# Weight remainders of an odd projection on VectorE, a decay root without a reciprocal, and modulation panels streamed at other places

## The reference, cut to what matters

```python
def sublayer(x, shift, scale, gate, g_pre, g_post, fn):          # 4 of them: two layers, mixer and feed-forward
    h = rmsnorm(x, g_pre) * (1 + scale[:, None]) + shift[:, None]
    return x + gate[:, None] * rmsnorm(fn(h), g_post)

shift, scale, gate, ... = split(silu(cvec) @ mod_w[l] + mod_b[l], 6)   # 2 x (1024 x 6144)

# layer 0: h @ w_in_even (1024 x 3072) -> qa ka va qb kb vb; differential attention (a) and
#          neighbourhood attention (b), both with 128 cached keys; @ w_out_even; SwiGLU (2816)
# layer 1: h @ w_in_odd (1024 x 3088) -> q k v o gates xd gd
q, k = split(silu(conv_centred(qk, conv_c)), 2)
hc = rmsnorm(mlstm(q, k, v, gates), norm_g) * sigmoid(o)         # 4 heads, forward and backward
xc = conv_centred(xd, conv_d) + conv_d_b
# rglru(xc), forward and backward:
r  = sigmoid(xb @ wa + ba);  ig = sigmoid(xb @ wx + bx)
log_a = -8 * r * softplus(-lam);  a = exp(log_a)
u = sqrt(-expm1(2 * log_a)) * (ig * x)
h[t] = a[t] * h[t-1] + u[t]
out = concat([hc, (rf + rb) * gelu(gd)]) @ w_out_odd             # then a mixture of 8 SwiGLU experts, top 2
```

## Time and profile before

| | |
|---|---|
| three runs | 1744.79 us median, 1743.28 to 1745.66 |
| profiled execution | 1746.09 us, of it span 1744.5 |
| busy | TensorE 1512.4 us (87%), VectorE 1068.0 (61%), ScalarE 861.6 (49%), GpSimd 161.1 (9%) |
| DMA | 414.50 MB, 238 GB/s on average |
| even projection | 49 to 197.6 us; TensorE ends panel qa at 70, ka at 86.9, va at 104.2 |
| attention, its output projection | 197.6 to 320.3; 333 to 374 |
| up and down projection | 391 to 677 |
| odd projection | 686 to 877.5; the RG-LRU starts its scans' roots at 754 |
| mLSTM units | 877.5 to 928.5 |
| head norm, output projection | 928.5 to 941.4; 941.4 to 985.2 |
| router and experts | 1038 to 1744 |

### The profile page before, as it was taken

How to read it: one execution, slowest core, us unless ns; L and a number is a source line. 1 busy time by engine, 2 the same in 40 slices (tenths; PEclk the granted TensorE clock), 3 DMA queues, 4 the chain that set the end, 5 groups by cost and what they waited for, 6 DMA issues and landing times.

```text
span 1744.5 us, 18824 instructions
## 1 busy us (share of the span) xinstructions
PE 1512.4 (87%) x7288; PEld 1221.6 (70%) x7288; DVE 1068.0 (61%) x1254; ACT 861.6 (49%) x979; POOL 161.1 (9%) x184
## 2 busy tenths in 40 slices
PE   3877879889999996767776879999999999999992
PEld 1857535549999785756553468888888888888881
DVE  1412453443332435558854369889879889898894
ACT  2412234433232334353322357777767768777773
POOL 2200240000000002622300020000000000000001
PEclk8888989999999998888878989999999999999996
DMA  9952689433334232311210359999999999999993
GB/s 327 358 210 97 225 284 383 146 97 97 123 119 145 97 121 97 104 54 49 79 38 5 145 222 352 390 365 399 389 375 401 379 375 398 380 371 394 387 386 142
DMA packets 146619, 414.50 MB, mean 238 GB/s; under 512 B 6924, under 2 KB 30888, under 8 KB 146408
## 3 DMA queue, kind: packets, MB, share of 16 engines
q1 hardware_dynamic: 134192, 375.93, 57.9%
q0 software_dynamic: 9600, 34.07, 5.3%
q10 hardware_dynamic: 2744, 3.36, 0.6%
HBM read 391.29 MB, written 22.95 MB: 237 GB/s over the span
## 4 chain that ended last, share of the span: by engine, by line
PE 74%; DVE 13%; ACT 5%; DMA 5%; issue 2%; POOL 1%; ACTq 0%; POOLq 0%; DVEq 0%; SPq 0%
PE bank L1734 37%; PE bank L1503 10%; PE bank L1355 5%; PE bank L1514 5%; PE bank L1309 5%; DMA ring<-in_w_in_even_dram 3%; PE bank L1252 2%; DVE arena L2066 2%; PE bank L1441 2%; PE bank L1306 2%; DVE arena L2090 1%; PE bank L1471 1%; PE bank L1702 1%; DVE arena L2100 1%; PE bank L1458 1%
## 5 line engine op out<-in xcount | busy, mean ns | idle before, releaser
L1734 PE MATMUL bank<-arena_parts 128*128 128x512 f32 x1520 | 399.9, 391 | 0.9 <-DVE arena_parts L2321 0.9
L1734 PEld LDWEIGHTS bank<-arena_parts 128*128 128x128 f32 x1520 | 283.7, 188 | 62.2 <-issue 2.4
L2314 DVE TENSOR_TENSOR ring_parts<-ring,arena_parts 128x2048 fp32r<-128x2048 f32 x124 | 278.4, 2285 | 71.0 <-ACT arena_parts L1154 70.9
L1154 ACT ACTIVATE arena_parts<-ring 128x2048 fp32r<-128x2048 f32 x124 | 234.5, 1920 | 31.0 <-DMA ring<-in_moe_w_dram 29.4
L1734 PE MATMUL bank<-ring_parts,arena_parts 128*128 128x512 f32 x720 | 222.5, 390 | 0.0
L1734 PEld LDWEIGHTS bank<-ring_parts,arena_parts 128*128 128x128 f32 x720 | 135.4, 188 | 28.5
L1503 PE MATMUL bank<-ht_parts,arena_parts 128*128 128x384 f32 x352 | 118.2, 336 | 0.4 <-DVE xn_parts L1834 0.3
L1503 PE MATMUL bank<-ht_parts,ring_parts 128*128 128x384 f32 x352 | 117.6, 334 | 0.0
L1503 PE MATMUL bank<-xn_parts,arena_parts 128*128 128x384 f32 x352 | 117.6, 334 | 0.0
L1734 PE MATMUL bank<-xn_parts,arena_parts 128*128 128x512 f32 x320 | 93.2, 393 | 7.5 <-DVE ring_parts L2314 7.5
L1734 PE MATMUL bank<-ht_parts,arena_parts 128*128 128x512 f32 x320 | 94.0, 395 | 0.0
(11 more groups left out here) (409 smaller groups left out, 2743.7 us busy)
## 6 DMA issues: line engine op xcount, KB each, us to landing
ring<-in_moe_w_dram SPq DMA_DIRECT2D x184, 1024.0 KB, 7.1
arena<-in_moe_w_dram SPq DMA_DIRECT2D x60, 1024.0 KB, 6.9
ring<-in_mod_w_dram SPq DMA_DIRECT2D x24, 2048.0 KB, 9.5
ring<-in_ff_w_dram SPq DMA_DIRECT2D x23, 1024.0 KB, 7.8
ring<-in_w_in_even_dram SPq DMA_DIRECT2D x6, 2048.0 KB, 15.4
ring<-in_w_in_odd_dram SPq DMA_DIRECT2D x6, 2048.0 KB, 8.0
ring<-in_ff_w_dram SPq DMA_DIRECT2D x5, 2048.0 KB, 8.0
routed<-arena POOLq DMA_DIRECT2D x1, 7168.0 KB, 25.5
```

What stands on the lines that cost most here:

```text
L1154: act.activation(whi_moe[n_ % E_WHI], e_half(j, h), ACT.Copy).then_inc(whi_ready, 1)
L1734: ins = pe.matmul(bank[base + b][:, :], lhs[:, c_, :], rhs[:, k, 512 * b:512 * b + 512], start=(first and h == 0 and k == 0 and n_ == 0), ...
L2314: dve.tensor_tensor(e_half(j, h, low=True), e_half(j, h), whi_moe[(2 * j + h) % E_WHI], ALU.subtract).then_inc(wlo_ready, 1)
```

## The change

1. **Panels.** mod 4 to 15 all come behind in0_5 and run in attention units 0 to 23; mod 16 to 23 come behind in1_5 and run in the eight mLSTM units, matmuls of panel 16 + u at the end of unit u and its transposes in unit u + 1. Units 24 to 35 of attention carry none. The PSUM banks change with it: panels from 16 on use bank 3, so the decay row has bank 2 alone and waits for the logs of the unit before. `gate_row(2)`, its copies and the last `add_mod` stand behind the last unit.
2. **Low parts.** VectorE makes those of w_in_odd; `low_quarter` moves there with the parts spread over its program. GpSimd keeps the three memsets, one behind the other.
3. **Decay root.** 1 - a^2 = (1 + a^2) tanh(L): ScalarE squares a between Exp and Tanh, and VectorE makes the product in one operation. The root loses its factor of 2.
4. **ScalarE's order.** The last high parts come earlier among the SiLUs, the softplus's exponential ahead of the v and o items.

```diff
             panels.append((("in0", j), [("k512", cut(I["w_in_even"][0], 512 * j, 512))]))
-            if j in (2, 3):
-                panels.append(mod_panel(2 + j))
-        panels += [mod_panel(m) for m in range(6, 24)]
+        panels += [mod_panel(m) for m in range(4, 16)]
...
             panels.append((("in1", j), [("k512", cut(I["w_in_odd"][0], c_, 512))]))
+        panels += [mod_panel(m) for m in range(16, 24)]
...
         def mod_bank(m):
-            return 5 if m < 4 and m % 2 else 7
+            return (5 if m % 2 else 7) if m < 4 else 7 if m < 16 else 3
         def mod_at(i):
-            return 6 + i // 2 if i % 2 == 0 and i // 2 < 18 else None
+            return 4 + i // 2 if i % 2 == 0 and i < 24 else None
...
-            pool.wait_ge(x_ready, 6)
+            pool.wait_ge(roots_ready, 7)
             pool.memset(xdin[:, :, :], 0.0).then_inc(zeroed, 1)
-            low_quarter(0)
...
-            project(0, 2, "va", (first_gate_panel, lambda: mod_turn(4)))
-            project(0, 3, "qb", (lambda: mod_mm(5), lambda: mod_turn(5), lambda: turn_cache(0)))
+            project(0, 2, "va")
+            project(0, 3, "qb", (lambda: turn_cache(0),))
```

ScalarE, the RG-LRU and the mLSTM units:

```diff
-                act.wait_ge(rg_exps, 8 * d + 4)
+                act.wait_ge(rg_exps, 9 * d + 4)
+                act.activation(rgb[3][:, :, 1:1 + NPAD], rgb[2][:, :, 1:1 + NPAD], ACT.Square).then_inc(rg_exps, 1)
...
             for n_ in range(8):
-                if n_ == 4:
-                    high_quarter(1, 19)
+                if n_ in (2, 4, 6):
+                    high_quarter(1, 18 + n_ // 2)
...
                 act.activation(cout[:, q, :], bank[6 + q][:, 258:387], ACT.Copy).then_inc(cout_kept, 1)
+                keep_mod(16 + u)
```

TensorE, mLSTM units:

```diff
-                if u >= 2:
-                    pe.wait_ge(wlog_ready, u - 1)
+                if u:
+                    pe.wait_ge(wlog_ready, u)
-                pe.matmul(bank[2 + u % 2][:, 0:T], cst[0:36, sel_:sel_ + P], ...)
+                pe.matmul(bank[2][:, 0:T], cst[0:36, sel_:sel_ + P], ...)
...
                 if u + 1 < 8:
                     mlstm_logs(u + 1)
+                if u:
+                    mod_turn(15 + u)
...
                   .then_inc(mm_done, 1)
+                mod_mm(16 + u)
+            mod_turn(23)
+            pe.wait_ge(h_ready, 8)
+            pe.wait_ge(inter_kept, 16)
+            pe.wait_ge(cout_kept, 8)
+            for c_ in range(CONDS):
+                gate_row(2, c_)
+            pe.wait_ge(mod_added, 24)
```

VectorE, in the order of its program:

```diff
             for k in range(KD):
                 halves_of(2, k)
+                if k in (3, 5, 7):
+                    low_quarter(k // 2 - 1, 1)
...
+            for n_ in range(3, 6):
+                low_quarter(n_, 1)
...
                      cols[:, col["conv_d_b"] + m:col["conv_d_b"] + m + 1]).then_inc(xc_ready, 1)
+                low_quarter(6 + m, 1)
...
                 then(dve.tensor_tensor(u_, u_, xc[:, :, 1:1 + NPAD], ALU.mult))
-                dve.wait_ge(rg_exps, 8 * (d + 1))
-                then(dve.tensor_scalar(tmp, th, 1.0, None, ALU.add))
-                then(dve.reciprocal(tmp, tmp))
-                dve.tensor_tensor(th, th, tmp, ALU.mult).then_inc(rg_ratio, 1)
+                low_quarter(11 + 4 * d, 1)
+                dve.wait_ge(rg_exps, 9 * (d + 1))
+                dve.scalar_tensor_tensor(out=th, in0=tmp, scalar=1.0, in1=th, op0=ALU.add, op1=ALU.mult)\
+                   .then_inc(rg_ratio, 1)
+                low_quarter(12 + 4 * d, 1)
...
+            low_quarter(10, 1)
             rg_chain(0)
+            low_quarter(13, 1)
             for m in range(4):
                 odd_item(index[("q", m)])
+            low_quarter(14, 1)
             rg_chain(1)
+            low_quarter(17, 1)
...
                 conv(qkc[:, m, :], qkin[:, m, :], col["conv_c"] + m, 8, 0.0).then_inc(conv_ready, 1)
+                if m % 2 == 0:
+                    low_quarter(18 + m // 2, 1)
...
             log1p_of(t2, ff, b_, nm, lf)
+            low_quarter(22, 1)
+            low_quarter(23, 1)
...
                 if u + 1 < 8:
                     mlstm_weigh(u + 1)
+                if u:
+                    add_mod(15 + u)
```

More of the change, by code:

```diff
@@ L510, in mod_bank @@
         def mod_bank(m):
-            return 5 if m < 4 and m % 2 else 7
+            return (5 if m % 2 else 7) if m < 4 else 7 if m < 16 else 3
         def turn_bank(m):
-            return 4 if m < 4 else 7
+            return 4 if m < 4 else 7 if m < 16 else 3
         def gate_bank(s, c_):
-            return {0: (4, 6), 1: (4, 4), 2: (0, 2), 3: (6, 6)}[s][c_]
+            return {0: (4, 6), 1: (4, 4), 2: (4, 6), 3: (6, 6)}[s][c_]
         def mod_row(m):
-            return gb[:, m % 2, 0:512] if m < 6 else jk[:, m % 2, :]
+            return gb[:, m % 2, 0:512] if m < 4 else jk[:, m % 2, :]
         def mod_at(i):
-            return 6 + i // 2 if i % 2 == 0 and i // 2 < 18 else None
+            return 4 + i // 2 if i % 2 == 0 and i < 24 else None
         def turn_at(i):
-            return 6 + i // 2 if i % 2 == 1 and i // 2 < 18 else None
+            return 4 + i // 2 if i % 2 == 1 and i < 24 else None
         munits = [(h, d) for h in range(C_HEADS) for d in range(2)]
@@ L733, in _ @@
             pool.wait_ge(zeroed, 10)
-            for n_ in range(20, 24):
-                low_quarter(n_)
             pool.wait_ge(zeros_out, 32)
@@ L1062, in rg_chain @@
                 act.wait_ge(rg_ratio, d + 1)
-                act.activation(rgb[0][:, :, 1:1 + NPAD], rgb[0][:, :, 1:1 + NPAD], ACT.Sqrt, scale=2.0)\
+                act.activation(rgb[0][:, :, 1:1 + NPAD], rgb[0][:, :, 1:1 + NPAD], ACT.Sqrt)\
                    .then_inc(rg_root, 1)
@@ L1127, in _ @@
             head_norm(1)
+            keep_gates(2)
+            turned_heads(1)
             act.wait_ge(fin_turned, 1)
@@ L1378, in turn_cache @@
                 else:
[L1379 removed]
+                    wait_kept(pe, index[("qa", 3)])
                 for h in range(4):
@@ L1475, in _ @@
             pe.wait_ge(o_kept, NU)
-            pe.wait_ge(mod_added, 24)
+            pe.wait_ge(mod_added, 16)
             for c_ in range(CONDS):
@@ L1572, in _ @@
             wait_kept(pe, index[("o", 0)])
-            for c_ in range(CONDS):
-                gate_row(2, c_)
             pe.wait_ge(rows_m, 1)
@@ L1597, in mlstm_logs @@
                     ins.then_inc(st_done, 1)
-                if u >= 2:
-                    pe.wait_ge(wlog_ready, u - 1)
+                if u:
+                    pe.wait_ge(wlog_ready, u)
                 sel_ = C_SEL + (4 * d + h) * P
-                pe.matmul(bank[2 + u % 2][:, 0:T], cst[0:36, sel_:sel_ + P], rwork[:, 6, :], start=True, stop=True)\
+                pe.matmul(bank[2][:, 0:T], cst[0:36, sel_:sel_ + P], rwork[:, 6, :], start=True, stop=True)\
                   .then_inc(nm_done, 1)
@@ L1624, in _ @@
                   .then_inc(mm_done, 1)
+                mod_mm(16 + u)
[6 more added lines that the diff above has]
+            pe.wait_ge(mod_added, 24)
+            pe.wait_ge(heads_ready, 2)
+            turn_heads(1)
             pe.wait_ge(fin_ready, 8)
             pe.wait_ge(rg_free, 1)
-            pe.wait_ge(cout_kept, 8)
+            pe.wait_ge(gb_kept, 6)
             for a in range(2):
@@ L1788, in shifts @@
                 dve.scalar_tensor_tensor(out=acol[:, s, :, :], in0=modc[:, l, h + 8:h + 16, :], scalar=1.0,
-                                         in1=g(s, 0), op0=ALU.add, op1=ALU.mult).then_inc(shifts_ready, 1)
+                                         in1=norm_gain(s, 0), op0=ALU.add, op1=ALU.mult).then_inc(shifts_ready, 1)
             def gains(s):
@@ L1817, in hidden_lo, with low_quarter @@
                 dve.tensor_tensor(fl[f % F_RING], actt[:, f, :], fh[f % F_RING], ALU.subtract).then_inc(fl_ready, 1)
-            def low_quarter(n):
-                _, hi, src, lo = quarter(0, n)
-                dve.wait_ge(whq_ready, n + 1)
+            def low_quarter(n, o=0):
+                _, hi, src, lo = quarter(o, n)
+                dve.wait_ge(whq_ready, 24 * o + n + 1)
                 dve.tensor_tensor(lo, src, hi, ALU.subtract).then_inc(wlq_ready, 1)
@@ L1918, in _ @@
                 low_quarter(n_)
-            add_mod(4)
-            for n_ in range(16, 19):
-                low_quarter(n_)
-            add_mod(5)
-            for n_ in range(19, 24):
+            for n_ in range(16, 24):
                 low_quarter(n_)
@@ L2236, in _ @@
                     mlstm_logs(u + 2)
+            add_mod(23)
             dve.wait_ge(h_ready, 8)
```

31 lines of the change are left out of this document (5 added, 26 removed).

## The result

The changed kernel takes 1684.12 us (median of 4 runs, 1680.32 to 1689.88) against 1745.19 (1743.28 to 1745.66): ratio 0.9655, interval 0.962 to 0.969. Two later series of six runs each (`after_again`, `after_third`) gave medians of 1681.0 and 1680.61. The forecast was 1693, in a range of 1679 to 1712.

The account below looks back on a forecast made before the run. Bound by stretch: w_in_even panel waits in even projection, TensorE in attention, mostly VectorE in odd projection, neither full in mLSTM units. Terms -36.5 - 10 - 18 + 12 = -52.5 from 1746.09 gave 1693.6; forecast 1693, range 1679 to 1712.

Parts of the forecast that it names:

- Part 1: Even projection: panels 4 and 5 leave, exposed waits for w_in_even go, -36.5 us; bounds 30 and 38.
- rival c: Even projection: zero fill holds in0_3 and ScalarE past 104 us, one transfer of 14 stays exposed: 1707, chance 0.05.
- Part 2: Attention: 12 panels, not 18; emptied units at 1.8 us, less one for the clock: -10 us, bounds 6 and 14.6.
- Parts 3 and 4: Odd stage to first mLSTM matmul: low parts on VectorE and new decay root, -18 us; bounds -10 and -26.
- the late start: Odd projection: memsets block the first casts, so the first matmul comes 3.5 us later; about +4 with three gaps.
- The kinder bound of 18: Decay root, both directions: 14.0 us saved, bounds 12 and 18, the 18 with Square and low part hidden.
- the terms for the softplus, `gb`, the parts among the convolutions and 22 and 23: Odd stage: softplus unstretched -4.0, no mLSTM wait for `gb` -2.0, convolution parts net +2, low parts 22 and 23 +2.4.
- Rival (b): Odd projection: VectorE becomes the bound, 30 us of low parts land on the chain, no gain: 1711, chance 0.08.
- Part 5: mLSTM units: eight panels make periods 6.3 and 7.6 us against 5.2, a loss of +12; bounds +9 and +27.
- Rival (a): mLSTM stage: new waits keep TensorE cold at 1.2 GHz, +27 there: 1708 in all, chance 0.07.
- (d): mLSTM units: panels come late, mean period past some 13 us, slower than before: 1750, chance 0.02.

Follow-up runs that it names:

- lows_only: Kernel before with only the low parts of w_in_odd on VectorE and ScalarE's order for them: 1738.18 us, ratio 0.9963.
- root_only: Kernel before with only the decay root replaced, low parts still on GpSimd: 1735.49 us, ratio 0.9947.
- panels_only: Kernel before with only the new panel order, banks and units: 1711.91 us, ratio 0.9804.
- early_22: Kernel after with high parts 22 and 23 ahead of the last SiLU, their low parts ahead of the softplus series: 1676.4 us, ratio 0.9614.
- scan_beside: Kernel after with low parts 13 and 17 put back on GpSimd, beside the scans: 1689.84 us, ratio 0.9694.
- rows_first: Kernel after with unit u + 2's scores and decay row ahead of unit u's modulation matmuls on TensorE: 1679.65 us, ratio 0.9657.
- turn_late: rows_first plus a panel's transposes behind the unit's output matmuls and its copy behind the next exponential: 1675.22 us, ratio 0.961.
- best16: Kernel after with early_22 and turn_late together: 1673.25 us, ratio 0.9597.
- att18: Kernel after with panels 4 to 21 in all 36 attention units, only 22 and 23 in mLSTM units: 1679.4 us, ratio 0.9639.
- best18: best16 with 18 panels in attention and two in the mLSTM units: 1676.0 us, ratio 0.9604.

## Why the prediction was right, and where it was off

**Part 1, -36.5.** Measured -39.1 in this pair of profiles, 1 us beyond the kinder bound. The transfers' waits vary by themselves: `lows_only` and `root_only`, whose even stage is that of before, reach attention at 195.0 and 194.3, and against these the gain is 36. Mechanism and size stand; the zero fill held nothing up (rival c).

**Part 2, -10.** Measured -4.2, outside the bounds of 6 to 14.6. The units without panels did run at 1.8 us (three of them from the scores at 250.92 to those at 256.38) until 262 us; then the granted clock fell to 0.50 and stayed there past the last of them. The term that failed is the clock: one microsecond was taken for it, and between the two profiles compared here it is 5.8. It is not paid each time. In the profile of `after_third`, the same code, the window over the same units stays at 0.99, and the stretch to the output projection takes 125.3 us (-10.0, the forecast to the tenth, though that forecast had a microsecond for the clock in it):

```profile
247.00:272.00 25.00, 21.56 (x123) 15.08 (x122) 12.22 (x58) 12.40 (x40) 0.00 (x0) 0.99 0.24 79
```

The nine profiles whose last twelve units carry no panel fall into two groups. In four (`after`, `after_again`, `panels_only`, `early_22`) the granted clock from 264 to 270 us is 0.50 and the stretch takes 130.8 to 131.2 us; in five (`after_third`, `scan_beside`, `rows_first`, `turn_late`, `best16`) it is 1.00 there and the stretch takes 123.4 to 125.3. In the five profiles whose units all carry panels (`before`, `lows_only`, `root_only`, `att18`, `best18`) it held at 1.00 to the last scores. So the emptier TensorE goes with the fall; what makes the clock fall in one execution and not in another was not found.

**Parts 3 and 4, -18 with the late start.** Measured -26.3 (3.7 later, 30.0 shorter). By its steps: the late start of the first matmul was put at 3.5 and is 3.7. The low parts take 1.22 to 1.24 us on VectorE, as priced. The roots, without the scans, gave 29.7 - 8.0 = 21.7 to 18.3 - 3.95 = 14.4, so 7.3 in the first direction, against 7.0. (The kinder bound of 18 is not what its words say: with Square and low part both hidden, twice 10.8 would go, 21.6.) The first direction started 0.6 us earlier net of the late first matmul, where 2.5 were forecast, and behind the scans of the second 1.7 went, where the terms for the softplus, `gb`, the parts among the convolutions and 22 and 23 make 1.6. The term that was not there at all is the scans, 4.1 us in each direction, and it is about the whole difference. The rows that tell it, shown above, could be read in the trace of before: two of eight scans at 2.45 and 2.75 us, with sisters of 0.39 and 0.72. The prediction looked for stretched operations among casts and the softplus only, and left the 8.01 us of the group as they were. Rival (b), VectorE as the bound, was wrong for the same reason: in `lows_only`, which adds the subtractions and takes nothing else off, VectorE's busy time over the whole is 1063.0 us against 1068.0. With the root changed too, its busy time in the stage fell from 135.1 to 102.3 us.

**Part 5, +12.** Measured +10.6, with periods of 6.08 and 7.36 for 6.3 and 7.6. Rival (a) did not come: the clock in the units rose from 0.77 to 0.89. Nor did (d): the chain through the units holds no wait for a panel.

**The sum.** -52.5 was forecast and -58.5 measured: two errors of opposite sign, the scans (8.2 us more gain) and the clock (5.8 less), then 2.6 more from the even stage and 1.4 less loss in the units. The steps that the prediction names for its five parts all show in the profiles, except the clock in attention and the scans, which it mis-sized or did not have; that these two errors, the largest, had opposite signs was luck.

**The spread.** The sixteen runs of the kernel after lie between 1674 and 1692 us. Three of them have a profile, and these differ by two switches. One is the clock above. The other is a matter of hundredths of a microsecond: the start of VectorE's first convolution tap in q and k (a tensor_scalar) against GpSimd's DMA issue and, behind it, its memset of the gate rows. In the profile of the kernel after, the tap starts 0.03 us ahead of the issue (VectorE's timeline and GpSimd's):

```profile
754.79 0.41 DVE L2050 TENSOR_SCALAR arena<-arena,cols 128x387 f32<-128x387 f32 x1
...
758.23 1.39 DVE L2050 TENSOR_SCALAR arena<-arena,cols 128x387 f32<-128x387 f32 x1
```

```profile
754.82 0.93 POOL L714 DMA_DIRECT2D arena<-in_state_c_C_dram  x1 [81.65 <-PE bank L1539]
```

In that of `after_again` it starts ahead by less than 0.02 us; VectorE's timeline and GpSimd's:

```profile
754.87 4.81 DVE L2050 TENSOR_SCALAR arena<-arena,cols 128x387 f32<-128x387 f32 x1
```

```profile
754.88 0.93 POOL L714 DMA_DIRECT2D arena<-in_state_c_C_dram  x1 [81.67 <-PE bank L1539]
755.80 3.66 POOL L716 MEMSET arena<- 36x4224 f32 x1
```

4.81 us for 0.41, till the memset is over, and the odd projection took 162.2 us instead of 158.8. `turn_late` and `best16` show the same, 4.81 us at less than 0.02 us ahead; in the six profiles with 0.41 us the tap starts 0.03 to 0.05 us ahead. With both switches well placed the profiled execution took 1681.33 (`after_third`), with the clock alone against it 1687.67, with both 1691.52. That the other thirteen runs divide by these two is not shown: `after_again` falls into two groups (1680.36 to 1681.57, and 1691.52 and 1692.16), but `after_third`, of which two groups were expected, has one run at 1674.46, four from 1679.63 to 1682.1 and one at 1689.53. Moving the memset was not tried.

## What to carry to other kernels

When work moves off GpSimd, look in the trace of before for groups whose members differ: a two-input VectorE operation that starts while a GpSimd part runs can hold hidden time, and its group mean is then no price for the kernel after. A part's gain measured alone is no share of the whole here: a shorter root alone pushed its neighbours into GpSimd's way, met a lower clock in the units, and kept half of its expected gain. When an in-order engine is given filler work, put what the other engines wait for ahead of it, and put the filler's own waits behind; that order was worth 6 of 10.6 us. And where the attention units carried filler, TensorE's clock held in all five profiles, without it in five of nine; so taking filler out may give back less than its own time.

## What had not been expected of the hardware

A single-input tensor_scalar of 0.41 us took 4.81 beside a DMA issue and a memset on GpSimd, while the two-input operations behind the first tap in the kernel after (L2052, 0.63 to 0.65 each) ran beside the same memset at their usual pace. A VectorE reciprocal of 128x1548 took 9.83 or 9.84 us with and without GpSimd beside it. GpSimd lost time too where it started second: 2.98 to 3.12 us for a part of 2.4 behind the start of a 1.77 us operation, and 3.90 behind the stretched multiply.
